# Two of the four token differences of the feed-forward products, made by GpSimd

## The reference, cut to what matters

```
h = rms_norm(x, norm_ffn_pre[i])
gate, up = split_cols(h @ w_ffn_in[i], (D_FF, D_FF))     # D_FF = 2816
f = (jax.nn.silu(gate) * up) @ w_ffn_out[i]
x = x + rms_norm(f, norm_ffn_post[i])
```

## Time and profile before

| | us |
|---|---|
| median of 3 runs | 1246.45 (1246.43 to 1246.53) |
| profiled execution | 1246.74 |
| its span, first to last instruction | 1244.90 |
| around the span | 1.84 |
| PE busy | 1236.6 |
| DVE busy | 786.8 |
| ACT busy | 571.7 |
| GpSimd busy | 131.3 |

### The profile page before, as it was taken

The page is one execution under the profiler, slowest core; times in us unless marked ns, Lnnn a source line. Parts: engine busy times, 40 slices in busy tenths (PEclk is TensorE's granted clock), DMA queues, the critical chain, the costliest instruction groups (busy, mean ns, idle before and its releaser), DMA issues.

```text
span 1244.9 us, 20535 instructions
## 1 busy us (share of the span) xinstructions
PE 1236.6 (99%) x8045; PEld 1136.7 (91%) x8045; DVE 786.8 (63%) x1329; ACT 571.7 (46%) x1084; POOL 131.3 (11%) x225
## 2 busy tenths in 40 slices
PE   9999999999999999999999999999999999999998
PEld 7999888999999988888899989889999999888886
DVE  5575545888888843337466746368988887532463
ACT  6444334555555532235454444263655555322351
POOL 2003521100000000002120037120000000000020
PEclk9999999999999999999999999999999999999999
DMA  7322132233333353322232222231333332523211
GB/s 248 104 65 89 69 102 68 69 102 102 102 108 112 104 170 102 131 72 89 77 96 62 89 65 85 85 97 57 102 108 112 105 103 102 170 85 134 68 51 67
DMA packets 124206, 122.30 MB, mean 98 GB/s; under 512 B 5200, under 2 KB 109008, under 8 KB 124112
## 3 DMA queue, kind: packets, MB, share of 16 engines
q1 hardware_dynamic: 124112, 121.01, 31.2%
HBM read 118.90 MB, written 2.10 MB: 97 GB/s over the span
## 4 chain that ended last, share of the span: by engine, by line
PE 99%; DVE 0%; DMA 0%; SPq 0%; issue 0%; ACT 0%; ACTq 0%
PE bank L800 30%; PE bank L802 30%; PE bank L801 30%; PE bank L993 2%; PE bank L1050 1%; PE bank L1073 1%; PE bank L1119 1%; PE bank L1071 1%; PE bank L1103 1%; PE bank L1058 0%; PE bank L1095 0%; PE bank L1115 0%; DMA raw<-in_w_in 0%; PE bank L1124 0%; PE bank L1145 0%; PE bank L1032 0%
## 5 line engine op out<-in xcount | busy, mean ns | idle before, releaser
L800 PE MATMUL bank<-w_hi,h_hi 128*128 128x384 f32 (+2 forms) x672 | 244.0, 363 | 1.8 <-DVE w_lo L1605 1.8
L801 PE MATMUL bank<-w_lo,h_hi 128*128 128x384 f32 (+2 forms) x672 | 237.5, 353 | 0.0
L802 PE MATMUL bank<-w_hi,h_lo 128*128 128x384 f32 (+2 forms) x576 | 200.4, 348 | 0.0
L1603 DVE TENSOR_TENSOR w_lo<-raw,w_hi 128x1024 fp32r<-128x1024 f32 x86 | 102.4, 1230 | 150.0 <-ACT w_hi L1189 149.8
L1189 ACT ACTIVATE w_hi<-raw 128x1024 fp32r<-128x1024 f32 x86 | 86.7, 1055 | 174.5 <-PE bank L802 174.4
L800 PE MATMUL bank<-h_hi,w_hi 128*128 128x256 f32 x568 | 161.0, 284 | 0.5 <-issue 0.5
L802 PE MATMUL bank<-h_hi,w_lo 128*128 128x256 f32 x568 | 160.7, 283 | 0.0
L801 PE MATMUL bank<-h_lo,w_hi 128*128 128x256 f32 x568 | 160.7, 283 | 0.0
L800 PEld LDWEIGHTS bank<-w_hi,h_hi 128*128 128x128 f32 x672 | 126.4, 188 | 15.5 <-issue 1.7
L802 PE MATMUL bank<-w_hi,mid_lo 128*128 128x512 f32 x352 | 137.0, 389 | 0.0
L801 PEld LDWEIGHTS bank<-w_lo,h_hi 128*128 128x128 f32 x672 | 126.6, 188 | 10.7
(11 more groups left out here) (235 smaller groups left out, 2665.6 us busy)
## 6 DMA issues: line engine op xcount, KB each, us to landing
raw<-in_w_ffn_in SPq DMA_DIRECT2D x88, 512.0 KB, 3.8
raw<-in_w_ffn_out SPq DMA_DIRECT2D x44, 512.0 KB, 3.3
raw<-in_w_in SPq DMA_DIRECT2D x40, 384.0 KB, 3.7
raw<-in_w_out SPq DMA_DIRECT2D x16, 512.0 KB, 4.0
raw<-in_w_gate SPq DMA_DIRECT2D x16, 512.0 KB, 4.1
raw<-in_w_in SPq DMA_DIRECT2D x10, 512.0 KB, 4.1
raw<-in_w_ple SPq DMA_DIRECT2D x4, 512.0 KB, 5.1
x<-in_x_in SPq DMA_DIRECT2D x3, 512.0 KB, 6.9
```

Of the source, the lines that this page charges most:

```text
L800: pe.matmul(out_ap, a_hi, b_hi, start=start, stop=False, skip_group_check=True)
L801: pe.matmul(out_ap, a_hi, b_lo, start=False, stop=False, skip_group_check=True)
L802: return pe.matmul(out_ap, a_lo, b_hi, start=False, stop=stop, skip_group_check=True)
L1603: last = dve.tensor_tensor(lo, raw[q % RAWS][:, cols], hi, ALU.subtract)
```

## The change

T3 and T4 of both halves are no longer made by DVE but by GpSimd, as plain `tensor_tensor` subtractions of the same 128x512 blocks. They stand at the same events, ("diff", p, 1). GpSimd waits until T2 of its half is written. They count on a semaphore of their own, `t_diff`, 4 per layer; `t_raw` now counts 4 per layer. ACT waits on `t_diff` before `T_hi` 2 and 3, and DVE waits for all four before its second `T_lo`, which overwrites T2. The rest of every engine's order is as before.

```diff
@@ -952,7 +953,7 @@
                     elif m == 0:
-                        pe.wait_ge(t_raw, 8 * layer + 2)
+                        pe.wait_ge(t_raw, 4 * layer + 2)
@@ -1268,7 +1269,10 @@
                 elif kind == "Tc":
                     for i in range(4):
-                        act.wait_ge(t_raw, 8 * layer + 5 + i)
+                        if i < 2:
+                            act.wait_ge(t_raw, 4 * layer + 3 + i)
+                        else:
+                            act.wait_ge(t_diff, 4 * layer + 1 + i)
                         act.activation(T_hi[:, i, :, :], T_sum[:, i, :, :], ACT.Copy).then_inc(t_hi, 1)
@@ -1504,6 +1508,13 @@
+                elif kind == "diff" and e[2]:
+                    p = e[1]
+                    pool.wait_ge(t_raw, 4 * layer + 2 * p + 2)
+                    cols = slice(p * P, (p + 1) * P)
+                    t2, t3, t4 = (T_sum[:, i, :, cols] for i in (1, 2, 3))
+                    pool.tensor_tensor(t3, t2, h_raw[:, 0, :, cols], ALU.subtract).then_inc(t_diff, 1)
+                    pool.tensor_tensor(t4, h_raw[:, 1, :, cols], t2, ALU.subtract).then_inc(t_diff, 1)
@@ -1670,19 +1681,14 @@
-            def differences(layer, p, part):
+            def differences(layer, p):
 
                 cols = slice(p * P, (p + 1) * P)
                 top, low = (banks[4 + 2 * p + i][:, :].rearrange("p (k t) -> p k t", k=4) for i in range(2))
-                t1, t2, t3, t4 = (T_sum[:, i, :, cols] for i in range(4))
-                if part:
-                    landed(combos["T2"])
-                    done(dve.tensor_tensor(t3, t2, h_raw[:, 0, :, cols], ALU.subtract), t_raw)
-                    done(dve.tensor_tensor(t4, h_raw[:, 1, :, cols], t2, ALU.subtract), t_raw)
-                    return
+                t1, t2 = (T_sum[:, i, :, cols] for i in range(2))
@@ -1758,11 +1764,13 @@
-                elif kind == "diff":
-                    differences(layer, e[1], e[2])
+                elif kind == "diff" and not e[2]:
+                    differences(layer, e[1])
                 elif kind == "Tc":
-                    dve.wait_ge(t_raw, 8 * layer + 8)
+                    dve.wait_ge(t_raw, 4 * layer + 4)
                     for i in range(4):
+                        if i == 1:
+                            dve.wait_ge(t_diff, 4 * layer + 4)
                         dve.wait_ge(t_hi, 4 * layer + i + 1)
```

More of the change, by code:

```diff
@@ L547, in build_trunk @@
     t_raw = sem("t_raw")
+    t_diff = sem("t_diff")
     t_hi = sem("t_hi")
@@ L1671, in _ @@
             combos = {}
-            def differences(layer, p, part):
+            def differences(layer, p):
                 cols = slice(p * P, (p + 1) * P)
                 top, low = (banks[4 + 2 * p + i][:, :].rearrange("p (k t) -> p k t", k=4) for i in range(2))
-                t1, t2, t3, t4 = (T_sum[:, i, :, cols] for i in range(4))
-                if part:
-                    landed(combos["T2"])
-                    done(dve.tensor_tensor(t3, t2, h_raw[:, 0, :, cols], ALU.subtract), t_raw)
-                    done(dve.tensor_tensor(t4, h_raw[:, 1, :, cols], t2, ALU.subtract), t_raw)
-                    return
+                t1, t2 = (T_sum[:, i, :, cols] for i in range(2))
                 dve.wait_ge(h_raw_ready, 4 * layer + 2 * p + 2)
                 landed(done(dve.tensor_tensor(t1, top, h_raw[:, 0, :, cols], ALU.subtract), t_raw))
-                combos["T2"] = done(dve.tensor_tensor(t2, low, t1, ALU.subtract), t_raw)
+                done(dve.tensor_tensor(t2, low, t1, ALU.subtract), t_raw)
             def combo(layer, name, j):
```

## The result

The changed kernel takes 1251.87 us, the median of 5 runs (1250.68 to 1252.40), against 1246.45 before: a ratio of 1.0041, 95% interval 1.003 to 1.0052. It is slower by 5.4 us. The profiled execution took 1250.75 us, with a span of 1249.0, 4.1 us longer than before, and GpSimd is busy for 144.9 us instead of 131.3.

A forecast was written before the change was run, and what follows sets the result against it. PE was taken to bound the kernel, waiting on DVE's first w_lo of f2; removal 0 plus four GpSimd turns of 1.17 us, 4.7, on 1246.45 gave 1251.1 us, range 1248.6 to 1252.6.

The forecast's parts named there:

- What bounds the kernel; the one wait that counts: PE, busy 99%, bounds; DVE's first w_lo of strip f2 sets PE's time there, a 0.49 us loss per layer.
- The removal at 0: Taking four subtractions, 2.4 us per layer, off DVE gains 0, since PE's own blocks hide it.
- The length of a GpSimd subtraction: A 128x512 subtraction with two plain inputs takes 1.40 us on GpSimd, with 1.06 kept for the range.
- The turns: Ahead of w_lo of f2, two GpSimd subtractions per layer get in between DVE instructions, delaying PE 2.34 us per layer.
- The first rival: At the two xn, DVE's queued instruction wins and GpSimd stays out; time 1246.4 us; chance 9%.
- What lies behind: After PE's wait, the second GpSimd pair and the waits on the new semaphore cost 0, with 1.5 us cover.
- The sum: 2 layers x 2 instructions x 1.17 = 4.7 us, so 1246.45 + 4.7 = 1251.1 us.
- The rival of the clock: After PE's idleness at f2 the clock falls to 1.2 GHz, up to 2.9 us more per layer: 1257; chance 5%.

The follow-up runs named there:

- late: The changed kernel, but GpSimd asks for its first pair of subtractions only when both halves of w_lo of f2 are written; 1246.35 us, ratio 1.0.
- half1: The changed kernel with only the second half's T3 and T4 on GpSimd, the first half's back on DVE; 1246.58 us, ratio 1.0.
- half0: The changed kernel with only the first half's T3 and T4 on GpSimd, the second half's back on DVE; 1251.29 us.
- the repeat: The changed kernel run once more, unaltered, on one chip beside the kernel with PE's wait filled by matmuls; 1251.19 us.
- dvework: The kernel before, GpSimd left alone, with two dummy DVE subtractions of 128x860 ahead of w_lo of f2 in each layer; 1252.39 us.
- twice: The changed kernel with each of the two GpSimd subtractions of the first half made twice, so four follow T2; 1252.20 us.
- filled: The changed kernel with 14 matmuls, whose result is overwritten, put into PE's wait for w_lo of f2; 1250.75 us.

## Why the prediction was right, and where it was off

- *What bounds the kernel; the one wait that counts.* Right. The whole change in the span lies in PE's step to f2 in the two layers, and `late` removes it by moving two instructions.
- *The removal at 0.* Right: `late` and `half1` have DVE relieved of 2.4 and 1.2 us per layer and are no faster.
- *The length of a GpSimd subtraction.* 1.40 us forecast, 1.30 to 1.31 measured. The term was mis-sized by 0.1: the line through 130 and 256 columns was too steep. The estimate by the Trainium skill's page (GPSIMD Engine Reference, Performance versus the Vector engine), 1.33, was nearer, and the measurement decides for it.
- *The turns.* Right in kind, place and number: one between the two `xn`, one between `xn` and `w_lo`. Each costs 1.04 to 1.07 us, the GpSimd length less 0.25, where 0.23 was read from the earlier trace rows. Two of them make 2.11 us a layer, where 2.34 was forecast, and PE's step came out at 3.40 us, not 3.62. The first rival, that DVE's full queue keeps GpSimd out, came in none of the profiles.
- *What lies behind.* Right. DVE waits for T4 of the second half, ends its last `T_lo` at 240.62 + 3.50 = 244.12 (244.65 forecast), and the product `mid` starts only at 245.83, behind ScalarE's `silu_g`, with 1.72 us to spare:

```profile
240.62 3.50 DVE L1775 TENSOR_TENSOR T_lo<-T_sum,T_hi 128x1024 fp32r<-128x1024 f32 x3 [1.18 <-POOL T_sum L1517]
245.83 0.69 DVE L1887 TENSOR_TENSOR mid<-silu_g,bank 128x512 f32<-128x512 f32 x1 [1.72 <-ACT silu_g L1375]
```

- *The sum.* By the measured turns it is 1246.45 + 4.2 = 1250.7, and two of the five runs lie there (1250.68, 1250.75). The forecast's 1251.1 was 0.4 over it, nearly all from the length.
- *The rival of the clock.* This is the step that failed in its chance and its size, not in its kind. It was given 5% and taken as all or nothing, at 2.9 us a layer. It came in about half of the runs of the change, `half0` and the repeat together (7 of 15 lie over 1251.8), for about 1.5 us a time. The median of the change fell on that side, so 1251.87 is 4.2 us of turns and about 1.2 us of what follows from PE's idleness. That the forecast of 1251.1 is only 0.8 off is in part luck: a GpSimd length too long and a clock price left out have opposite signs, and with the length right it would have been 1.2 off. That the upper runs of the change itself had a fallen clock is inferred from `half0`, `dvework`, `twice`, `filled` and the mean clocks on record; none of its own upper runs was profiled.

## What to carry to other kernels

Before work is moved from VectorE to GpSimd, look at what VectorE runs from the moment the moved work may start: if those instructions have two SBUF inputs and a saturated engine waits for one of them, each GpSimd instruction that reads SBUF puts most of its length in front (here 1.05 of 1.30 us). A wait that holds GpSimd back until VectorE comes to PSUM work makes it free, and work that was behind the wait anyway brings nothing when it is moved. And a stall of TensorE may cost more than its own length: price the matmuls behind it at the lower clock in part of the runs.

## What the runs showed of the hardware that was not expected

- After idle times of only 0.5 and 1.6 us, the granted clock fell to 0.50 for 3.4 us in some executions, and in others behind the same idle times it didn't; `dvework`, with one idle time of 2.4 us ahead, had it too. In the three profiles that have it, it fell 0.1 to 0.6 us after PE had taken up work again, not during the idleness. With the 1.6 us filled by matmuls, five of five runs were free of it by their times.
- GpSimd at 128x512 in float32: a subtraction takes 1.30 us where VectorE takes 0.68; a memset takes 0.53.
- Neither engine starves the other: with four GpSimd instructions queued against four of VectorE, three got in between them, one at a time, and the fourth followed (`twice`: the two `xn` 2.44, the two `w_lo` 4.50 us).
